# TensorE's program aligned once per pair of heads to a fixed place in a block of 256 instructions

## The reference

```
def step(s, inp):
    w_t, k_t, v_t, a_t, b_t = inp[:5]
    sa = jnp.einsum("bhvk,bhk->bhv", s, a_t)
    s = s * w_t[:, :, None, :] + sa[..., None] * b_t[:, :, None, :] + v_t[..., None] * k_t[:, :, None, :]
    y = jnp.einsum("bhvk,bhk->bhv", s, inp[5]) if emit else None
    return s, y
```

## Time and profile before

| | |
|---|---|
| median of 3 runs | 2350.02 us |
| the profiled execution | 2346.09 us |
| its span, first to last instruction | 2344.2 us |
| TensorE busy (matmul) | 2285.3 us, 97% |
| VectorE, ScalarE, GpSimd busy | 52%, 50%, 57% |
| mean granted TensorE clock | 0.995 |
| the eight pairs, about | 147 to 762 us |

### The profile page before, as it was taken

One profiled execution on the slowest core, in us unless ns is written; L12 is line 12 of the kernel. 1 busy time (PEld: TensorE's weight loads), 2 busy tenths in 40 slices (PEclk: granted clock), 3 DMA queues, 4 the chain that ended last, 5 costly groups with the idle time before them and its releaser, 6 DMA issues.

```text
span 2344.2 us, 60261 instructions
## 1 busy us (share of the span) xinstructions
PE 2285.3 (97%) x23364; PEld 1944.4 (83%) x23364; DVE 1223.2 (52%) x2449; ACT 1178.7 (50%) x1999; POOL 1342.1 (57%) x566
## 2 busy tenths in 40 slices
PE   6999999999999999999999999999999999999997
PEld 4787787778777888899999888888888888888886
DVE  2478778877883323466565455453444533333322
ACT  3244545454554444444444555555555555555554
POOL 1112123212332344478888878777777877778785
PEclk8999999999999999999999999999999999999999
DMA  9922112211211223267776555555555555555553
GB/s 389 381 87 66 40 60 77 66 41 58 70 65 50 81 99 108 99 222 251 256 252 244 183 166 176 168 173 173 177 172 171 181 169 172 177 177 172 170 181 134
DMA packets 101244, 360.70 MB, mean 154 GB/s; under 512 B 11184, under 2 KB 14768, under 8 KB 101072
## 3 DMA queue, kind: packets, MB, share of 16 engines
q1 hardware_dynamic: 99872, 356.89, 44.4%
q10 hardware_dynamic: 1200, 1.25, 0.2%
HBM read 356.00 MB, written 2.10 MB: 153 GB/s over the span
## 4 chain that ended last, share of the span: by engine, by line
PE 89%; DVE 2%; ACT 2%; issue 1%; DVEq 0%; ACTq 0%
PE ps L223 32%; PE ps L224 16%; PE ps L684 5%; PE ps L196 4%; PE ps L198 4%; PE ps L197 4%; PE ps L686 4%; PE ps L685 4%; PE ps L815 1%; PE ps L800 1%; PE ps L836 1%; PE ps L980 1%; PE ps L850 1%; PE ps L951 1%; PE ps L1000 1%
## 5 line engine op out<-in xcount | busy, mean ns | idle before, releaser
L187 POOL TENSOR_TENSOR wlo<-raw,whi 128x1024 fp32r<-128x1024 f32 x555 | 1336.7, 2422 | 948.7 <-ACT whi L178 898.7
L223 PE MATMUL ps<-acts,whi 128*128 128x512 f32 x3072 | 1087.6, 398 | 1.3 <-DVE acts L2794 1.3
L224 PE MATMUL ps<-acts,wlo 128*128 128x256 f32 x3072 | 856.7, 279 | 0.0
L178 ACT ACTIVATE whi<-raw 128x1024 fp32r<-128x1024 f32 x562 | 591.6, 1054 | 267.1 <-PE ps L224 138.3
L223 PEld LDWEIGHTS ps<-acts,whi 128*128 128x128 f32 x3072 | 576.2, 188 | 131.6 <-DVE acts L2794 1.6
L224 PEld LDWEIGHTS ps<-acts,wlo 128*128 128x128 f32 x3072 | 579.0, 188 | 0.9
L684 PE MATMUL ps<-acts,whi 128*128 128x512 f32 (+1 forms) x560 | 216.9, 387 | 0.9 <-DVE W L1560 0.9
L686 PE MATMUL ps<-acts,wlo 128*128 128x512 f32 (+1 forms) x560 | 190.1, 339 | 0.0
L685 PE MATMUL ps<-acts,whi 128*128 128x512 f32 (+1 forms) x560 | 189.8, 339 | 0.0
L196 PE MATMUL ps<-acts,whi 128*128 128x256 f32 (+1 forms) x576 | 181.7, 315 | 0.0
L198 PE MATMUL ps<-acts,wlo 128*128 128x256 f32 (+1 forms) x576 | 180.0, 313 | 0.0
(11 more groups left out here) (391 smaller groups left out, 3087.8 us busy)
## 6 DMA issues: line engine op xcount, KB each, us to landing
raw<-stream SPq DMA_DIRECT2D x564, 512.0 KB, 3.3
W<-stream SPq DMA_DIRECT2D x64, 512.0 KB, 9.1
graw<-stream SPq DMA_DIRECT2D x32, 512.0 KB, 4.3
W<-xT SPq DMA_DIRECT2D x4, 1024.0 KB, 8.7
XR<-xT SPq DMA_DIRECT2D x16, 128.0 KB, 5.7
outT<-XR SPq DMA_DIRECT2D x4, 512.0 KB, 3.3
cns<-consts SPq DMA_DIRECT2D x1, 928.0 KB, 11.1
cns<-consts SPq DMA_DIRECT2D x1, 896.0 KB, 7.4
```

What stands on the lines that cost most here:

```text
L178: nc.scalar.activation(high, raw[slot], ACT.Copy).then_inc(hi_done, 1)
L187: nc.gpsimd.tensor_tensor(wlo[slot], raw[slot], whi[slot].bitcast(F32), ALU.subtract).then_inc(lo_done, 1)
L223: nc.tensor.matmul(both_parts, whi[slot][:, k, :], hl[:, :, k0 + k, :], start=first and k == 0, stop=False)
L224: ins = nc.tensor.matmul(ps[:, bank, 0:T], wlo[slot][:, k, :], hl[:, 0, k0 + k, :], start=False, stop=last and k == UK - 1)
```

## The change

One line is added in `pe_inverse`, behind the second `square` and its two pieces:

```
--- before.py
+++ after.py
@@ -890,6 +890,7 @@
             apart(pe)
             square(AL, BE, 4).then_inc(R["prod_a"].sem, 1)
             fill(2)
+            pe.addr_align(256, offset=100)
             R["ka_ok"].wait(pe, i + 1)
             R["zc"].wait(pe, i + 1)
             if i:
```

## The result

The change made the kernel slower by 3.3%: 2426.55 us median of 5 runs (2424.71 to 2432.63) against 2351.47 us for the kernel before on the same chip (5 runs), ratio 1.0328, 95% interval 1.0315 to 1.0341. The profiled execution took 2426.55 us against 2346.09, 80.5 us more.

The account below looks back on a forecast made before the run. TensorE, 97% busy, was taken as the bound, held at late instruction blocks. Fills 40 us, clock 8 and places 0 made 48 on 2346.1, 2394 profiled, 2398 us as median; forecast's own range 2375 to 2430, wider range 2349 to 2442.

Parts of the forecast that it names:

- Late blocks at every 256th instruction, and the pairs' places: TensorE's program comes in 256-instruction blocks, some late (0.54 to 0.81 us idle); place is L116's slot in its block.
- One sign: Expected in the trace after the change: idle times within L800 and L836 at the same instruction in every pair.
- Number of fills: NOPs put in ahead of the place: 99 in each of pairs 1 to 7, 210 in pair 0, 903 in all.
- What one costs: A NOP on TensorE's sequencer, between 8.5 and 100 ns: taken as 50 ns; fills with cover deducted 40 us.
- dear fills: Rival: a NOP costs 100 ns, start to start, giving 99 us more with the clock, 2449 us; chance 0.10.
- What they hide behind: Sequencer 1.65 us ahead of the array at the place: 1.4 us cover, of which 0.35 us per pair is kept.
- The border ahead of the fills: In pairs 1 to 7, a block border directly ahead of the NOPs: waiting for the block eats most of the lead.
- The clock: Half clock behind pauses in pair 0 and every second other pair, 1.7 us each: 8 us, between 0 and 14.
- The places: All pairs at place 100, judged by pair 3 at place 96, 77.24 us against the mean 77.23: counted as 0.
- The rest: Behind the pairs the program and its borders shift by 144 slots: counted as 0, 2 us either way.
- Cheap fills: Rival: NOPs pass at the weight loads' 8.5 ns, 2353 us, or at 17 ns, 2360 us; chance 0.20.
- the place helps: Rival: cheap fills and place 100 clears the late block, -8 us and +3 for the fills, 2345 us; chance 0.08.

Follow-up runs that it names:

- branch38: Directive with offset 38 and a branch over the filling instructions (max_nops=0), against the kernel before: 2364.57 us, ratio 1.0066.
- fill48: Place 195 in all pairs, reached by a branch and then 48 fills run through, against the kernel before: 2366.20 us, ratio 1.0070.
- fill99: Place 195 in all pairs, reached by a branch and then 99 fills run through, against the kernel before: 2411.72 us, ratio 1.0264.
- branch100: The change's place 100, but with a branch over the filling instructions (max_nops=0), against the kernel before: 2345.27 us, ratio 0.9983.
- order_only: The kernel before with only VectorE's long product moved behind state(5), no directive, against the kernel before: 2348.16 us, ratio 0.9986.
- branch195: Directive with offset 195 and a branch over the filling instructions (max_nops=0), against the kernel before: 2345.40 us, ratio 0.9979.
- order195: branch195 with VectorE's long product moved behind state(5), ratio against the kernel before: 2342.81 us, ratio 0.9971.

## Why the prediction was right or wrong

It forecast 2398 us, and slower; measured were 2426.55 us. The direction and the cause were found: the fills, at a price far over the weight loads', beyond the sequencer's lead, and the clock on top. The sizes were too small, the price of a fill above all.

- *Late blocks at every 256th instruction, and the pairs' places.* Right in the main: branch38 brings two of pair 1's three idle times into every pair from 1 on. One sign did not come: in the change's own trace no idle time stands within L800 or L836.
- *Number of fills.* 903 forecast, 912 measured. Pair 0 has no head sums and is 9 instructions shorter, so pair 1 gets 108 fills. 0.7 us.
- *What one costs.* This term was the mis-sized one. I took 50 ns, the duration of a semaphore instruction; measured are 13 ns of duration, but 75 ns from start to start. The row that was nearer stood in the same group: two neighbouring sequencer instructions 0.1 to 0.2 us apart. What counts in a row of them is the distance of starts, as I had written under the rival *dear fills* and not followed. Fills: 40 us forecast, 59.7 us of pause measured. At 75 ns, and with the clock's 1.7 us in all eight pairs, the prediction's own sum would be 7 x 7.08 + 13.1 + 13.6 = 76 us, or 2426. That it meets the measured time so closely is partly luck: the pauses are 3 us shorter than in it, and the clock took 6 us more.
- *What they hide behind.* 1.4 us of lead forecast; 1.6 hidden in fill48, 1.9 in fill99. The border ahead of the fills was given 1.05 us of it per pair; pauses 0.6 to 1.7 us longer than fill99's, 0.9 in the mean, agree, but the border was not isolated.
- *The clock.* Forecast for pair 0 and every second other pair at 1.7 us, 8 us; it fell in every pair, and cost 15.9 us in pairs 0 to 6 and 4.1 in pair 7. The lower bound of none is out, and the upper one of 14 was too low. In five pairs the size was right: 6.8 us at half clock, of which some 3.3 are work. In pairs 0, 5 and 7 it was 9 us of work, 3.7 to 4.4 us lost each.
- *The places.* 0 forecast; branch100 puts them at 4 us of gain (2.8 of it within the pairs by the traces). I took pair 3 at place 96 for all pairs, with its late block of 0.54 us; at 100 some pairs have it and some have not.
- *The rest.* Of the 80.5 us between the profiled executions, 75.4 had come by the last small product of the pairs. They are 59.7 of pauses, 20.0 of clock and a first pair that starts 1.05 us later, less some 5 us of other idle time: "issue" apart from the pauses fell from 6.7 to 3.3 us, and the 1.25 us for VectorE in pair 0 went, as forecast. Behind the pairs it is 5.1 us more, but in order_only, where nothing of TensorE's program is changed, 4.5 more than before: the shift there, counted as nothing, is not resolved.
- *Rivals.* Cheap fills are out (75 ns, not 8.5 or 17). Dear fills, 2449 us at 100 ns, were nearer (22 us off) than the forecast (29 us off), with the fills priced too high instead of too low. That the place helps is true in small, but only once the fills are not run through.

The Trainium skill, Runtime: NRT & Kernel Launch, Instruction fetch mechanics, calls the fetching of instructions hidden. Here it is not: branch38 shows 11.2 us of idle time within L800 alone, at products that the place sets, and branch195 none there.

## What to carry to other kernels

Price a row of sequencer instructions from start to start, not by their duration, and set it against the lead of the sequencer over the array at that point: behind large products 16 fills were free, 99 cost 5.5 us and the clock on top. If a place in a block is worth keeping, branch to it, from within the same block, or spread the fills; then look which other engines the freed time brings together. An idle time put down to "issue" may still be another engine's: compare the same instruction's duration from pass to pass.

## What the runs showed of the hardware that had not been expected

- A NOP on TensorE's sequencer takes 75 ns from start to start and shows as 13 ns. The branch that replaces them shows as 170 ns where it stays in its block (view of the new line in branch195), but as 1.9 to 2.8 us where it leads over a border (all pairs of branch38, pair 0 of branch100 and of fill99). In pair 1 of branch100, where it starts 8 slots short of the border, it shows as 0.69 us:

```profile
L893 PEldq COMPARE_BRANCH  x8: 170/170/191, 151.0 to 692.6; - x8
```

- VectorE's 128x1024 product and GpSimd's 128x1024 subtraction hold each other: 1.21 and 3.45 us, or 3.42 and 2.37 us, as GpSimd's starts 10 or 30 to 40 ns ahead. A gain of 1 us earlier in a pair can so be lost behind it.
- With pauses of 5.5 us and more the granted clock was at half (1.2 GHz) in every pair, for 3.4 to 20 us, part of the pause included; behind pauses of 2.0 us in two of eight. The length of the pause alone does not decide: it was at half for 3.4 us behind the idle time of 1.2 us in pair 0 of order195 too. In pair 0 of the change it was at 0.50 for the whole stretch behind a pause of 13.9 us:

```profile
167.20:176.40 9.20, 9.20 (x87) 0.50 0.01 2
```
